# Shared-expert steps between the gate and up products, last norms on two engines, turned tiles one by one, 18 units in the first mixture's loop

## What is computed

```python
def moe_ffn(h, ...):                      # first block, 16 experts, two per token
    for e in range(N_EXPERTS):
        a = jax.nn.silu(h @ w_gate[e]) * (h @ w_up[e])
        y = y + combine[:, e:e + 1] * (a @ w_down[e])

def hier_moe(h, ...):                     # second block, 64 experts, two per token
    def expert_block(args):
        hid = jax.nn.silu(xb @ w_gate[e]) * (xb @ w_up[e])
        return hid @ w_down[e]
    ys = (jax.nn.silu(xt @ ws_gate) * (xt @ ws_up)) @ ws_down
    y = y + jax.nn.sigmoid(xt @ w_sg) * ys

h = rmsnorm(x, norm_w[i, 0]) * (1.0 + sc1) + sh1      # input of the next mixer
```

## Time and profile before

| | |
|---|---|
| median of 3 runs | 2866.75 us (2863.1 to 2868.97) |
| the profiled execution | 2866.93 us, of which the span is 2865.0 us |
| TensorE busy | 2246.7 us (78%) |
| VectorE busy | 1303.3 us (45%) |
| ScalarE busy | 846.6 us (30%) |
| DMA | 668.44 MB, mean 233 GB/s |
| mean granted TensorE clock | 0.90 |

### The profile page before, as it was taken

One profiled execution on the slowest core, in us unless ns is written; L12 is line 12 of the kernel. 1 busy time (PEld: TensorE's weight loads), 2 busy tenths in 40 slices (PEclk: granted clock), 3 DMA queues, 4 the chain that ended last, 5 costly groups with the idle time before them and its releaser, 6 DMA issues. The chain is left out here.

```text
span 2865.0 us, 43231 instructions
## 1 busy us (share of the span) xinstructions
PE 2246.7 (78%) x18058; PEld 1589.9 (55%) x18058; DVE 1303.3 (45%) x2046; ACT 846.6 (30%) x1378; POOL 194.2 (7%) x205
## 2 busy tenths in 40 slices
PE   5999998888993999866666756899979876666664
PEld 3877776886762788433333335677757533333332
DVE  3278877543223544532233345666544632233334
ACT  4177776312224323111111114434323311111111
POOL 2000000101001000100000000111110100000000
PEclk8999999988996999998888888999989988888887
DMA  7357765536983225799999952111113799899992
GB/s 278 93 191 232 238 222 187 102 149 227 326 303 133 88 89 192 309 389 363 393 402 381 371 215 81 52 45 39 40 58 118 271 378 387 362 390 369 374 384 110
DMA packets 210859, 668.44 MB, mean 233 GB/s; under 512 B 23693, under 2 KB 122710, under 8 KB 153814
## 3 DMA queue, kind: packets, MB, share of 16 engines
q1 hardware_dynamic: 195574, 625.04, 58.4%
q0 software_dynamic: 9648, 20.51, 2.1%
q10 hardware_dynamic: 5424, 19.93, 1.7%
HBM read 655.95 MB, written 23.62 MB: 237 GB/s over the span
## 5 line engine op out<-in xcount | busy, mean ns | idle before, releaser
L220 PE MATMUL PS<-second 128*128 128x256 f32 (+1 forms) x4944 | 940.9, 348 | 89.7 <-DVE second L250 54.6
L220 PE MATMUL PS<-ring,arena 128*32 128x256 f32 (+4 forms) x7424 | 750.8, 459 | 326.6 <-DMA ring<-in_moe_w_down 239.8
L220 PEld LDWEIGHTS PS<-second 128*128 128x128 f32 x4944 | 767.9, 195 | 242.4 <-DVE second L250 65.8
L220 PEld LDWEIGHTS PS<-ring,arena 128*32 128x32 f32 (+3 forms) x7424 | 389.0, 129 | 641.3 <-issue 474.3
L232 ACT ACTIVATE arena<-PS 128x512 f32<-128x512 f32 (+1 forms) x305 | 150.4, 493 | 796.3 <-PE PS L220 648.1
L220 PE MATMUL PS<-arena 128*64 128x64 f32 (+8 forms) x1728 | 302.5, 360 | 37.9 <-ACT arena L232 18.7
L220 PEld LDWEIGHTS PS<-arena 128*128 128x128 f32 (+4 forms) x1728 | 178.8, 173 | 142.3 <-issue 81.3
L250 DVE SCALAR_TENSOR_TENSOR second<-PS,arena,second 128x512 fp32r<-128x512 f32 x66 | 49.5, 751 | 440.0 <-ACT second L232 422.3
L239 DVE TENSOR_TENSOR second<-ring,second 128x1024 fp32r<-128x1024 f32 (+1 forms) x88 | 142.6, 1621 | 189.9 <-ACT second L232 184.8
L239 DVE TENSOR_TENSOR arena<-PS,arena 128x512 f32<-128x512 f32 x281 | 193.9, 690 | 72.5 <-PE PS L220 46.3
L232 ACT ACTIVATE second<-PS,arena 128x512 fp32r<-128x512 f32 x66 | 45.4, 687 | 594.1 <-PE PS L220 593.0
(11 more groups left out here) (160 smaller groups left out, 1223.5 us busy)
## 6 DMA issues: line engine op xcount, KB each, us to landing
ring<-in_moe_w_down SPq DMA_DIRECT2D x148, 1024.0 KB, 8.9
ring<-in_moe_w_up SPq DMA_DIRECT2D x146, 1024.0 KB, 10.1
ring<-in_moe_w_gate SPq DMA_DIRECT2D x140, 1024.0 KB, 13.3
ring<-in_ada_w SPq DMA_DIRECT2D x48, 1024.0 KB, 5.4
ring<-in_w_mod SPq DMA_DIRECT2D x24, 1024.0 KB, 6.8
ring<-in_gdn_in_w SPq DMA_DIRECT2D x32, 512.0 KB, 4.0
ring<-in_hg_w_in SPq DMA_DIRECT2D x24, 512.0 KB, 6.8
ring<-in_conv_in_w SPq DMA_DIRECT2D x12, 1024.0 KB, 5.2
```

What stands on the lines that cost most here:

```text
L220: return P.e.matmul(o, l, r, start=st, stop=sp)
```

## The change

1. **Place of the shared expert's steps.** In `gate_up_pe` one step is taken between the gate and the up product of a unit (`between`), and the rest right after the up product, ahead of `hidden_pe`. `SIDE` sets the counts: (1, 2, 1, 2, 2, 1, 2, 1, 0, 2, 2, 2, 2) for units 0 to 12, and none in 13 to 15. Unit 0 takes its step after the up product. VectorE and ScalarE advance their generators right behind their own part of gate and up. The loads of the shared expert move by a unit or so.
2. **Norms after the second mixture.** Tiles 1 and 3 are scaled by VectorE (`norm_x_ve`), tiles 0 and 2 by ScalarE as before. After the first mixture all four stay on ScalarE.
3. **Turned tiles one by one.** `transposed2_pe` takes its eight banks first, then waits for tile `t` alone and turns its eight blocks.
4. **First mixture's loop.** `NP` = 18 where `NS` is 16: the first two overflow units run in the loop, for any count. `extra_load` fetches their experts' matrices by a number read from memory. The branches begin at a count over 2.

```diff
-    def transposed2_pe(src, name, turn, *before):
-        P.wait_ge(*before)
-        for k in range(8):
-            b = take(turn, name, k)
-            for t in range(4):
-                i = tr(b[:, t * 128:(t + 1) * 128], src[:, t, k * 128:(k + 1) * 128])
-            i.then_inc(*P.mark("ps", name, k))
+    def transposed2_pe(src, name, turn, stage):
+        bs = [take(turn, name, k) for k in range(8)]
+        for t in range(4):
+            P.wait_ge(at("xn", stage, t))
+            for k in range(8):
+                i = tr(bs[k][:, t * 128:(t + 1) * 128], src[:, t, k * 128:(k + 1) * 128])
+                if t == 3:
+                    i.then_inc(*P.mark("ps", name, k))
...
+    def norm_x_ve(name, t):
+        V.wait_ge(at("sq2", name, t))
+        ts(XN[:, t, :], x[:, t, :], rs[:, 4 + t:5 + t], None, ALU.mult, None, "xn", name, t)
...
-            if i >= 2 and name is not None:
+            if i >= 2 and name is not None and (name == "m0" or i % 2 == 0):
                 norm_x(name, i - 2)
...
+            self.NP = self.NS + (0 if i else 2)
...
+    def extra_load(m, turn, n, ws):
+        S.wait_ge(at("ei", m.i))
+        for w in ws:
+            src = None
+            if not state["dry"]:
+                e = S.e.value_load(m.eii[0:1, n - m.NS:n - m.NS + 1], min_val=0, max_val=m.NE - 1)
+                src = m.weights[w][bass.ds(e, 1)].rearrange("a (p k) n -> p (a k) n", p=128)
+            load(turn, src, (8, 8, 2)[w], done_with(m, n, w), "m", m.i, n, w, 0)
...
+    SIDE = (1, 2, 1, 2, 2, 1, 2, 1, 0, 2, 2, 2, 2)
+
     def side_steps(n):
-        return 2 if n in (1, 3, 5, 12) else 1
+        return SIDE[n] if n < len(SIDE) else 0
...
-        for n in range(m.NS):
-            if m.shared and n in (2, 3, 4, 6):
-                piece_sp(m, {2: 4, 3: 5, 4: 6, 6: 7}[n])
-            if m.shared and n in (5, 9):
+        for n in range(m.NP):
+            if m.shared and 2 <= n <= 5:
+                piece_sp(m, n + 2)
+            if m.shared and n in (6, 8):
...
     def gate_up_pe(m, n, between=None):
...
             i.then_inc(*P.mark("ps", "gu", m.i, n, w))
+            if between and w == 0:
+                next(between, None)
...
-        for n in range(m.NS):
-            gate_up_pe(m, n)
+        for n in range(m.NP):
+            early = int(n > 0 and side_steps(n) > 0)
+            gate_up_pe(m, n, more if early else None)
+            for _ in range(side_steps(n) - early):
+                next(more, None)
...
             if m.shared and n:
                 combine_pe(m, n - 1)
-            for _ in range(side_steps(n)):
-                next(more, None)
...
-        transposed2_pe(XN, "c0", turn, at("xn", "m0", 3))
+        transposed2_pe(XN, "c0", turn, "m0")
...
-        transposed2_pe(XN, "hG", turn, at("xn", "m1", 3))
+        transposed2_pe(XN, "hG", turn, "m1")
```

More of the change, by code:

```diff
@@ L1473, in moe_load @@
     def moe_load(m, turn, n, ws, hs_=None):
+        if n >= m.NS:
+            extra_load(m, turn, n, ws)
+            return
         for w in ws:
@@ L1576, in turn_pe, with gate_up_pe @@
         i.then_inc(*P.mark("ps", "turn", m.i, n))
-    def gate_up_pe(m, n):
+    def gate_up_pe(m, n, between=None):
         turn = state["units"]
@@ L1733, in moe_pe @@
                 hidden_pe(m, n - 1)
-            if m.shared is None and n + 1 < m.NS:
+            if m.shared is None and n + 1 < m.NP:
                 turn_pe(m, n + 1)
@@ L1737, in moe_pe @@
                 down_pe(m, n - 1)
-            if m.shared and n + 1 < m.NS:
+            if m.shared and n + 1 < m.NP:
                 turn_pe(m, n + 1)
@@ L2050, in moe_ve @@
                 next(more)
-        for n in range(m.NS):
+        for n in range(m.NP):
             gate_up_ve(m, n)
+            for _ in range(side_steps(n)):
+                next(more, None)
             if m.shared and n == 0:
@@ L2067, in moe_ve @@
                 more_places_ve(m, n + 1)
-            for _ in range(side_steps(n)):
-                next(more, None)
         count = count_of(m, V)
-        hidden_ve(m, m.NS - 1)
+        hidden_ve(m, m.NP - 1)
         for _ in more:
             pass
-        down_ve(m, m.NS - 1)
+        down_ve(m, m.NP - 1)
         if m.shared:
-            combine_ve(m, m.NS - 1)
+            combine_ve(m, m.NP - 1)
         def one(n):
@@ L2103, in moe_ve, with after @@
         V.wait_ge(at("ev", ("row", m.i), 1), at("ev", "frow", 1) if m.i == 0 else None)
-        tiles_ve(mix, final if m.i == 0 else lambda t: post_ve(f"m{m.i}", t))
+        def after(t):
+            post_ve(f"m{m.i}", t)
+            if m.i == 1 and t == 3:
+                norm_x_ve("m1", 1)
+        tiles_ve(mix, final if m.i == 0 else after)
+        if m.i == 1:
+            norm_x_ve("m1", 3)
     def turn_ac(m, n):
@@ L2158, in moe_ac @@
         turn_ac(m, 0)
-        for n in range(m.NS):
+        for n in range(m.NP):
             gate_up_ac(m, n)
-            if n == m.NS - 1:
+            for _ in range(4 * (n == 0) + side_steps(n)):
+                next(more, None)
+            if n == m.NP - 1:
                 for _ in more:
@@ L2168, in moe_ac @@
                 down_ac(m, n - 1)
-            if m.shared and n + 1 < m.NS:
+            if m.shared and n + 1 < m.NP:
                 turn_ac(m, n + 1)
-            for _ in range(4 * (n == 0) + side_steps(n)):
-                next(more, None)
             if n == m.row_at:
@@ L2206, in gather_gp @@
     def gather_gp(m, n):
-        d = D(f"xg{n % 3}") if n < m.NS else state["over"][m.i][n - m.NS]
+        d = D(f"xg{n % 3}") if n < m.NP else state["over"][m.i][n - m.NS]
         G.wait_ge(at("idx" if n < m.NS else "idx2", m.i), at("xn_d", m.i), at("zx", m.i), at("ps", "turn", m.i, n - 3) if n > 2 else None)
```

19 lines of the change are left out of this document (10 added, 9 removed).

## The result

The changed kernel takes **2784.18 us** (median of 4 runs, 2780.03 to 2785.36), the kernel before beside it 2865.99 us: ratio 0.9712, 95% interval 0.9695 to 0.9729. The forecast was 2789 us, in a range of 2770 to 2828. The profiled execution took 2785.36 us, span 2783.3, mean granted clock 0.914.

A forecast was written before the change was run, and what follows sets the result against it. The second and third mixture's loops were taken as almost bound by the DMA engines, whose queue ran dry. From 2866.93 us, 62 + 11 + 4.6 = 77.6 us less gave 2789 us, range 2770 to 2828.

The forecast's parts named there:

- The dry queue and its cure: Second and third mixture: moving shared steps from between down and gate product keeps the load queue filled, 62 us less.
- t + 17.4: In a mixture unit, gate product's end without a shared step, 17.4 us after the down matrices are in.
- the 74 us: Second and third mixture: time in which the DMA engines have nothing to do, 35 us plus 39 us.
- the deductions: Taken off 74 us: 9 for dips at the up matrices' issue, 3 for the next router's small loads.
- The first rival: In the loops, more queued loads only stretch each load, so the dry time stays; 2851 us, chance 0.08.
- The second rival: In the loops, the queue runs dry behind the up product, leaving 31 of 62 us; 2820 us, chance 0.22.
- a margin of 1.2: Behind the gate product, four queued down matrices last 9.9 us against 8.7 us until the next gate matrices are issued.
- TensorE at its lower clock: Rival: waits at two places per unit keep the loops' clock low, TensorE becomes the bound; 2980 us, chance 0.04.
- First mixture: Two overflow units each cost a loop period of 11.8 us instead of 17.35, 11 us less.
- The sign of eighteen equal periods: Sign of being right: the first mixture has eighteen equal periods of 11.8 us.
- Tiles: Start of the gated-delta stage: norms on two engines and tiles turned one by one, 4.6 us less.
- Convolution: Convolution stage: turning tiles earlier gains nothing, since VectorE first forms a matrix's low part.

## Why the prediction was right

**The dry queue and its cure: right in mechanism and size.** 62 us were forecast. The loops gave 29.2 + 34.4 = 63.6 in the profiles, and the kernel with the steps alone was 64.7 us faster (67.6 in the loops of its profile). The issue of the next down loads was put at t + 17.4 and measured at 16.4 (the down product took 5.1 us of the 6.2 assumed). The share of 0.99, the two stages 29 and 34 us shorter and the short wait for up matrices behind the step are as listed beforehand. That the size fits to 2 us is in part luck. One hundredth of a share is 5 us in each loop, so the 74 us are known to some 10 us only; counted in pieces of 2 us they were 80. And the deductions stand in the wrong places: no dip is seen at the issue of the up matrices (share 1.02 from 1522 to 1524, not 0.84), while the first units, for which the sum took nothing off, still run dry. The small loads of the next router did cost something (share 0.83 from 1300 to 1310 us, and 11.6 us of waiting ahead of the down product at 1323.31, the longest such wait in the loop).

**The first rival (loads only stretched) is refuted:** the rate was 403 GB/s over 476 us, where it needed 380 to be the limit. The Trainium skill ("DMA: Bandwidth & Descriptors", section "Where 436 GB/s comes from") puts the limit between HBM and SBUF at about 358 GB/s; the trace, of one core at work, disagrees with these 403.

**The second rival (half comes back) rested on a mis-sized step.** The prediction set 8.7 us from the gate product to the next gate issue against the 9.9 us of the four down matrices, a margin of 1.2. But at that point the up matrices were still loading, until t + 21, so that the 9.9 us begin some 3.6 us later. The experiment with both steps there took this 1.2 us margin away with 3.6 us more, and the queue did not run dry in the unit read. The forecast came out right with a margin that was wrong, and the rival's 0.22 rested on it.

**TensorE at its lower clock: no.** The granted clock in the loops rose from 0.87 and 0.86 to 0.90. It still falls behind the waits for down matrices: 0.59 in the down product at 2315.99, behind 3.88 us, and 0.70 in the one at 1515.78, behind 2.41 us. The up products behind waits of 1.00 us (2304.60) and 1.63 us (1537.41) ran at 1.00, so the lower clock did not return after both waits. Where the second wait is longer, it does (3.60 us and then 5.35 us for 3.66, at 2689.04), under cover of loads.

**First mixture:** 11 us forecast, 10.8 in the profile, 9.2 (4 either way) alone. Over all profiles the second mixture's first gate load stands at 1072.6 to 1076.7 us in the three kernels with 16 units (mean 1074.2) and at 1062.1 to 1069.7 in the eleven with 18 (mean 1064.0), a difference of 10.2. The sign of eighteen equal periods was not met as put: the units' gate loads stand 11.8 us apart from 755.06 to 814.18 us, and up to 14.7 ahead of that, in both kernels. The gain asked only that the two added units take a period each, as they do.

**Tiles:** 4.6 forecast, 4.65 in the profile (4.2 behind the last square, 0.4 ahead of it), 3.4 (3 either way) alone. VectorE's scaling took 0.75 us, not 1.13, without effect: ScalarE's tile 2 is ready last, 2.9 us behind the start of the last square, as assumed. **Convolution:** nothing was forecast; no experiment has it by itself, and the norms and turning together gave no more than the 4.6 us of the other stage.

**Not forecast: 6.4 us less in the rest of the gated-delta stage, and some 4 us more ahead of the second mixture,** both in unchanged code (see the last section). Together they are 2.5 us less, so of the 4 us by which the profiles' 81.7 exceed the 77.6 forecast, 1.6 are the loops' and the rest is mostly this, which nobody forecast.

## What to carry to other kernels

Where a loop is nearly bound by its loads, ask at what time each load is issued and what stands on the releasing engine between the last arrival and that time. Work that isn't urgent belongs where the engine waits for data anyway, behind the products that release slots, not ahead of them. And count the queue from when its bytes really begin to move: what is queued ahead of a load is cover too.

## What the runs showed that was not expected

The gated-delta stage has the same instructions in all kernels, from VectorE's first taking out to the third mixture's read of `x_d`. Before, after, and with the steps alone:

```profile
1738.08:2186.91 448.83, 398.84 (x4294) 314.46 (x4294) 259.81 (x343) 167.12 (x234) 58.64 (x45) 0.92 0.17 46
```
```profile
1697.18:2139.59 442.41, 393.35 (x4294) 310.40 (x4294) 259.78 (x343) 167.19 (x234) 58.38 (x45) 0.94 0.17 48
```
```profile
1700.59:2142.09 441.50, 391.05 (x4294) 307.53 (x4294) 259.78 (x343) 167.13 (x234) 58.66 (x45) 0.95 0.17 47
```

The length goes with the granted clock: 441.5 us at 0.95, 442.3 to 442.6 at 0.94 (five profiles), 443.8 to 446.9 at 0.93 (six), 446.6 and 448.8 at 0.92. VectorE and ScalarE are busy for the same time in all, TensorE for 5.5 us less than before in the changed kernel. The norms and the turning are not the cause: the kernel with the steps alone, whose norms and turning wait as before, has the 6.4 us too, and the one with norms and turning alone has only 2.3. What moves the clock stays open, and the change can have a part in it. The four kernels with the old place of the steps lie at 445.1 to 448.8 us. Of the ten profiles with the new place seven lie at 441.5 to 443.8, the other three at 445.5 to 446.9. The two kernels that were profiled twice repeat within 0.3 us (442.41 and 442.33, 442.30 and 442.52). So a few us between single profiles in a stage that an edit leaves alone are neither to be credited to the edit nor to be called chance without more runs.

VectorE scaled a tile of 128x1024 in 0.75 us here, where the mean of the 18 such operations of the earlier trace rows is 1.13 and one ahead of the first mixture takes 1.23 (at 606.98 us in the changed kernel's profile). Those ahead of a mixture (`norm_mixed_ve`) read their input in another order of columns, `q (p k) -> q k p`, and write it in order; `norm_x_ve` does both in order. That this is the cause was not tried.
